# Order of the first block: softmax products ahead of the gate projections, spatial products sooner, six modulation pieces later

## The reference

```
h = rms_norm(x);  q, ckv, qi, ki, wi, u, v, ga, gb = split(h @ w_in)
index = sum_heads(relu(qi . ki) * wi)          # top 64 keys per query
scores = q_lat . c_kv * scale + bias, masked to the chosen keys
o = softmax(scores) @ values;  y_a = o @ w_proj_a
y_b = (gelu(u) * (w_spatial @ layer_norm(gelu(v)) + b_spatial)) @ w_proj_b
x = x + (sigmoid(ga) * y_a + sigmoid(gb) * y_b) @ w_out
x = x + mixture_of_32_experts(rms_norm(x))     # 96 MB of weights
```

## Time and profile before

| | us |
|---|---|
| median of 3 runs | 999.6 |
| lowest, highest | 999.0, 1003.27 |
| profiled execution, its own time | 995.97 |
| its span | 994.2 |
| PE busy | 914.5 (92%) |
| DVE busy | 406.0 (41%) |
| ACT busy | 261.5 (26%) |
| POOL busy | 66.9 (7%) |
| chain that ended last: PE, SP's queue, DMA, DVE | 78%, 10%, 4%, 4% |

### The profile page before, as it was taken

One profiled execution on the slowest core, in us unless ns is written; L12 is line 12 of the kernel. 1 busy time (PEld: TensorE's weight loads), 2 busy tenths in 40 slices (PEclk: granted clock), 3 DMA queues, 4 the chain that ended last, 5 costly groups with the idle time before them and its releaser, 6 DMA issues.

```text
span 994.2 us, 13560 instructions
## 1 busy us (share of the span) xinstructions
PE 914.5 (92%) x5310; PEld 729.6 (73%) x5310; DVE 406.0 (41%) x906; ACT 261.5 (26%) x588; POOL 66.9 (7%) x88
## 2 busy tenths in 40 slices
PE   8889998799999976876799999999999999999997
PEld 7658776688865544443588888788888888878886
DVE  4474555464631211111552461645135236263422
ACT  2244422201322111110327143122111814312201
POOL 5523100002000000000200000000000000000011
PEclk9979999899999988888899999999999999999999
DMA  9935956379999999999463444223334443422311
GB/s 347 371 128 218 374 214 237 143 312 422 371 421 420 422 420 421 421 420 421 165 180 139 168 143 154 103 110 127 128 127 143 175 152 145 169 85 93 136 48 43
DMA packets 35124, 229.52 MB, mean 231 GB/s; under 512 B 5984, under 2 KB 6016, under 8 KB 8176
## 3 DMA queue, kind: packets, MB, share of 16 engines
q1 hardware_dynamic: 30944, 222.05, 57.5%
q0 software_dynamic: 1312, 4.71, 1.3%
q10 hardware_dynamic: 2800, 1.85, 0.6%
HBM read 227.54 MB, written 1.06 MB: 230 GB/s over the span
## 4 chain that ended last, share of the span: by engine, by line
PE 78%; SPq 10%; DMA 4%; DVE 4%; ACT 2%; issue 2%; POOL 0%; DVEq 0%; ACTq 0%; POOLq 0%
PE bank L423 27%; PE bank L1023 11%; SPq L1048 9%; PE bank L886 6%; PE bank L864 6%; PE bank L728 3%; PE bank L629 3%; PE bank L906 3%; DMA s<-in_w_down 3%; PE bank L700 2%; PE bank L743 2%; PE bank L461 2%; PE bank L921 1%; PE bank L987 1%; PE bank L766 1%
## 5 line engine op out<-in xcount | busy, mean ns | idle before, releaser
L423 PE MATMUL bank<-hT,ring 128*128 128x256 f32 x1152 | 261.0, 386 | 1.6 <-DMA ring<-in_first_pieces 1.4
L423 PEld LDWEIGHTS bank<-hT,ring 128*128 128x128 f32 x1152 | 221.0, 194 | 37.1 <-issue 3.4
L1023 PE MATMUL bank<-ring,s 128*128 128x256 f32 x512 | 111.2, 379 | 0.0
L1023 PEld LDWEIGHTS bank<-ring,s 128*128 128x128 f32 x512 | 97.2, 190 | 13.0
L1719 DVE SCALAR_TENSOR_TENSOR z<-z,bank 128x256 f32<-128x256 f32 x9 | 3.8, 421 | 151.5 <-ACT z L1270 151.5
L728 PE MATMUL bank<-s,z 128*32 128x256 f32 (+1 forms) x448 | 45.6, 428 | 15.3 <-DMA s<-in_w_up 4.5
L886 PE MATMUL bank<-ring,hT 128*128 128x256 f32 x256 | 56.4, 380 | 0.0
L728 PE MATMUL bank<-ring,z 128*32 128x256 f32 (+1 forms) x336 | 40.9, 434 | 16.5 <-DMA oth<-in_w_up 6.7
L864 PE MATMUL bank<-hT,ring 128*128 128x256 f32 x256 | 55.6, 379 | 0.0
L886 PEld LDWEIGHTS bank<-ring,hT 128*128 128x128 f32 x256 | 48.4, 190 | 7.2 <-issue 0.9
L864 PEld LDWEIGHTS bank<-hT,ring 128*128 128x128 f32 x256 | 48.5, 190 | 6.5
(11 more groups left out here) (395 smaller groups left out, 1365.0 us busy)
## 6 DMA issues: line engine op xcount, KB each, us to landing
ring<-in_layer_pieces SPq DMA_DIRECT2D x64, 1024.0 KB, 4.8
ring<-in_first_pieces SPq DMA_DIRECT2D x49, 1024.0 KB, 7.4
s<-in_w_gate SPq DMA_DIRECT2D x15, 1024.0 KB, 17.5
s<-in_w_down SPq DMA_DIRECT2D x14, 1024.0 KB, 27.0
s<-in_w_up SPq DMA_DIRECT2D x13, 1024.0 KB, 13.4
ring<-in_w_up SPq DMA_DIRECT2D x11, 1024.0 KB, 19.9
ring<-in_w_gate SPq DMA_DIRECT2D x10, 1024.0 KB, 22.2
ring<-in_w_down SPq DMA_DIRECT2D x9, 1024.0 KB, 23.1
```

What stands on the lines that cost most here:

```text
L423: mm = pe.matmul(b[:, 0:T], w[:, (k0 + kb) * CW + m * P:(k0 + kb) * CW + (m + 1) * P], rhs[:, kb, :], start=(kb == 0), stop=(kb == nk - 1))
L1023: mm = pe.matmul(xo[j, tt][:, 0:CW], yT[:, kb, tt * P:(tt + 1) * P], w[:, kb, :], start=(kh == 0 and kb == 0), stop=(kh == 1 and kb == KB ...
```

## The change

The order of the pieces, the order of PE, ACT and DVE in the loop over heads, and one wait on POOL are changed. No arithmetic is added or taken away. The list of pieces now has no modulation piece behind the q pieces and two behind each v piece. PE does pT ahead of the gate halves of a head and o behind them; gm stands between pT of the last head and the last gate half. ACT copies pT ahead of the exps. DVE does its last modulation piece of the loop behind gmT. POOL waits until all 16 index scores have been added before it multiplies its first piece. ACT's sums of the six pieces move behind u and v.

```diff
--- before.py
+++ after.py
@@ -91,7 +91,9 @@
     tags = [("in", C_QI), ("in", C_QI + CW), left.pop(0), ("latent",), left.pop(0)]
     for c in (C_Q, C_U, C_V, C_GA, C_GB):
         for j in range(2 if c < C_GA else 4):
-            tags += [("in", c + j * CW), left.pop(0)]
+            tags.append(("in", c + j * CW))
+            for _ in range({C_Q: 0, C_U: 1, C_V: 2}.get(c, 1)):
+                tags.append(left.pop(0))
     for j in range(4):
         tags += [("proj", j), left.pop(0)]
     for j in range(4):
@@ -498,7 +500,6 @@
                     for _ in range(4):
                         idx_job()
                 used()
-                ada_job()
                 if j == 0:
                     pe.wait_ge(S["ckv_ready"], 1)
                     b = B.acquire(pe, "cT")
@@ -533,6 +534,7 @@
                     mm.then_inc(A.done, 1)
                 used()
                 ada_job()
+                ada_job()
 
             gate_jobs = [(j, m) for j in range(8) for m in range(2)]
             gst = {}
@@ -551,7 +553,6 @@
             for _ in range(GATES_FIRST):
                 gate_job()
             for h in range(HEADS + 1):
-                gate_job()
                 if h < HEADS:
                     o = (h % 2) * 64
                     for tt in range(TT):
@@ -559,11 +560,8 @@
                         b = B.acquire(pe, f"S{h}{tt}")
                         pe.matmul(b[:, 0:ns], qT[o:o + 64, h // 2, tt * P:(tt + 1) * P], kvT[o:o + 64, h // 2, 0:ns],
                                   start=True, stop=True).then_inc(B.done, 1)
-                if h < GATES_TWICE:
-                    gate_job()
                 if h >= 1:
                     g = h - 1
-                    o = (g % 2) * 64
                     pe.wait_ge(S["prob_ready"], 2 * g + 2)
 
                     b = A.acquire(pe, f"pT{g}")
@@ -571,6 +569,20 @@
                     tr(b[:, 0:P], pn[0][:, 0:P])
                     tr(b[:, P:2 * P], pn[1][:, 0:P])
                     tr(b[:, 2 * P:3 * P], pn[1][:, P:2 * P]).then_inc(A.done, 1)
+                if h == HEADS:
+                    pe.wait_ge(S["vln_ready"], 1)
+                    pe.wait_ge(S["ws_masked"], 1)
+                    for n in range(GROUPS):
+                        b = B.acquire(pe, f"gm{n}")
+                        for c in range(TT):
+                            mm = pe.matmul(b[:, c * P:(c + 1) * P], gv[:, c, n * P:(n + 1) * P], wsT[:, n, :],
+                                           start=True, stop=True)
+                        mm.then_inc(B.done, 1)
+                gate_job()
+                if h < GATES_TWICE:
+                    gate_job()
+                if h >= 1:
+                    o = (g % 2) * 64
                     pe.wait_ge(A.free, A.upto(f"pT{g}"))
                     b = A.acquire(pe, f"o{g}")
                     pe.matmul(b[o:o + 64, 0:P], vnat[:, 0, g * HD:(g + 1) * HD], pT[:, g % 2, 0, :],
@@ -580,15 +592,6 @@
                                        start=(st == 0), stop=(st == 1))
                     mm.then_inc(A.done, 1)
             assert not gate_jobs
-
-            pe.wait_ge(S["vln_ready"], 1)
-            pe.wait_ge(S["ws_masked"], 1)
-            for g in range(GROUPS):
-                b = B.acquire(pe, f"gm{g}")
-                for c in range(TT):
-                    mm = pe.matmul(b[:, c * P:(c + 1) * P], gv[:, c, g * P:(g + 1) * P], wsT[:, g, :],
-                                   start=True, stop=True)
-                mm.then_inc(B.done, 1)
 
             pe.wait_ge(B.free, B.upto("gm3"))
             pe.wait_ge(A.free, A.upto("o7"))
@@ -1171,8 +1174,6 @@
                 out_copy(qT[:, m, :], T)
                 for _ in range(4):
                     idx_job()
-                if m % 2:
-                    ada_job()
             act.wait_ge(S["sp_wanted"], 1)
             step(f(labs, labs, ACT.Exp, scale=-1.0), S["sp_ready"])
             for m in range(4):
@@ -1200,7 +1202,9 @@
             for _ in range(GATES_FIRST):
                 gate_job()
             for h in range(HEADS + 1):
-                gate_job()
+                if h >= 1:
+                    b = A.take(act)
+                    step(f(pT[:, (h - 1) % 2, :, :], b[:, 0:384].rearrange("p (s q) -> p s q", s=3), ACT.Copy), A.free)
                 if h < HEADS:
                     for tt in range(TT):
                         ns = (tt + 1) * P
@@ -1210,13 +1214,12 @@
                             act.wait_ge(A.done, A.upto(f"pT{h - 2}"))
                         step(f(prob[h % 2][tt][:, 0:ns], sc[:, tt, 0:ns], ACT.Exp, bias=rt[:, tt:tt + 1],
                                accum_out=rt[:, 2 + tt:3 + tt]), S["p_ready"])
+                gate_job()
                 if h < GATES_TWICE:
                     gate_job()
                 if h >= 1:
                     g = h - 1
                     o = (g % 2) * 64
-                    b = A.take(act)
-                    step(f(pT[:, g % 2, :, :], b[:, 0:384].rearrange("p (s q) -> p s q", s=3), ACT.Copy), A.free)
                     b = A.take(act)
                     step(f(oaT[o:o + 64, g // 2, :], b[o:o + 64, 0:T], ACT.Copy), A.free)
             assert not gates
@@ -1554,13 +1557,14 @@
                     step(tsc(pn, pn, rt[:, 4 + tt:5 + tt], None, ALU.mult), S["prob_ready"])
                 if h + 1 < HEADS:
                     masked_bias(h + 1)
-                ada_sums(1)
+                    ada_sums(1)
 
             for g in range(GROUPS):
                 b = B.take(v)
                 step(tten(gsum, b[:, 0:T].rearrange("p (c t) -> p c t", c=TT),
                           bsp[:, g, :].unsqueeze(1).broadcast_to([P, TT, P]), ALU.add))
                 step(tten(gmT[:, g, :], gsum.rearrange("p c t -> p (c t)"), guT[:, g, :], ALU.mult), B.free)
+            ada_sums(1)
 
 
             v.wait_ge(S["small_loaded"], 16 * 2)
@@ -2046,6 +2050,7 @@
             g.wait_ge(S["ws_loaded"], 16)
             step(g.affine_select(out=wsT, in_=wsT, compare_op=ALU.is_ge, fill=0.0, base=0,
                                  pattern=[[0, GROUPS], [1, P]], channel_multiplier=-1), S["ws_masked"])
+            g.wait_ge(S["relu_used"], 2 * HEADS)
             ada_sums(ADA_POOL)
             g.wait_ge(S["norm2_loaded"], 16)
             for j in range(4):
```

## The result

The changed kernel takes **984.1 us** (median of 4 runs, 980.9 to 986.2) against 1000.6 for the kernel before (4 runs, 999.0 to 1003.3): a ratio of 0.9829, interval 0.9805 to 0.9854. Its profiled execution took 984.0 us, with a span of 982.3. In a later batch two executions of the kernel before took 1102.1 and 1211.6 us, at a mean granted clock of 0.83 and 0.74 where all others have 0.96 to 0.98; these slow runs are left out of every ratio and median.

A forecast was written before the change was run, and what follows sets the result against it. The expert weight stream was taken to bound the kernel, following PE's first projection P. Shifts of -3.65 (V), +3.1 (supply), +1 (clock) and -14.8 (heads) gave 981.6 us profiled, with 3.6 added 985, range 978 to 993.

The forecast's parts named there:

- What bounds it: Expert stage is paced by its weight stream, which follows PE's first projection P; bringing P forward brings the rest forward.
- swallowed: Rival: the expert stream ends at 469 us whatever PE does, so the time stays at 999.6; chance 0.06.
- Index stretch: Index scores without POOL's multiplications: all 5.18 us of PE idle goes, last index addition moves from 65.15 to 58.2 us.
- One hold: Ahead of V, one POOL multiplication holds a small DVE instruction 4.5 us; V shifts -3.65 us; 985 us, chance 0.50.
- The case of two holds: Rival: a second multiplication also holds DVE's third small instruction, V starts 4.55 us later; 989.5 us, chance 0.27.
- V and u: PE's products V and u take 18.5 us as before, partly at half clock; u ends at 83.75.
- Supply: Before the heads: late loads of v's second and the second gate piece cost +3.1 us, plus +1 for the clock.
- Heads: Loop over heads up to P, reordered: 70.35 us instead of 85.17, so -14.8, ends -11 and -15.5.
- The sum: Whole kernel: -3.65 + 3.1 + 1 - 14.8 = -14.35, so 981.6 us profiled and 985 us median.
- the pieces' half: Moved modulation pieces with POOL's wait, everything outside the heads' reorder: terms -3.65, +3.1 and +1 us.
- The signs: Expected in the trace: POOL's first multiplication about 58.4, V near 65, DMA waits of 1 to 3 us, P near 180.
- the starved rival: Ring supply of v's second and gate pieces lands late, heads start 21 us later; slower, 1006 us, chance 0.05.

The follow-up runs named there:

- sp_wait: Changed kernel with POOL waiting for DVE's third small instruction (`sp_wanted`) instead of the 16th index addition: 976.7 us, ratio 0.9786 to the kernel before.
- pieces_only: Kernel before with only the six modulation pieces moved (new list, POOL's wait, ACT's sums behind u and v), heads' loop as before: 998.9 us, ratio 0.9994.
- lag0: Changed kernel with ACT summing each modulation piece in the call that first reaches it, not one later: 974.6 us, ratio 0.9729 to the kernel before.
- heads_exp_late: Kernel before with only the heads' loop reordered, and ACT's `sp_wanted` wait and small exp moved behind the copies of V: 982.1 us, ratio 0.9825.
- exp_late: Changed kernel with ACT's `sp_wanted` wait and small exp moved from before the copies of K to behind those of V: 971.1 us, ratio 0.9701.
- no_wait: Changed kernel without POOL's wait for the index additions: 979.9 us, ratio 0.9820 to the kernel before.

## Why the prediction was right

985.0 was predicted, 984.1 measured. The mechanism was right. That the two numbers lie so close is in part luck: the prediction worked out 981.6 us for the profiled execution and added 3.6, because the profile before lay that far under its median. The profiled execution took 984.0, so the sum was 2.4 too low; it lay only 0.1 under its median, so the addition was 3.5 too high. Point by point:

- **What bounds it.** P 15.8 us sooner, last landing 14.7 us sooner, median 16.5 us shorter, and over all thirteen profiles the rest keeps its length to some 4 us: the gain was not swallowed.
- **Index stretch.** Last index addition predicted at 58.2, ended at 58.41.
- **One hold.** Predicted: `sp_wanted` at 63.25, V at 65.25. Measured: 63.29, and V at 65.35. K's products end at 58.57 (58.35 predicted). It is the second small instruction that is held, as the sum had it, and the third got through between two multiplications. The case of two holds did not happen here, but sp_wait shows it elsewhere: L1517 and L1518, held by successive multiplications. By the rule of the Trainium skill weighed in the prediction ("SBUF — State Buffer", section "Who interferes with whom") either is possible; these traces show both.
- **V and u.** Predicted 18.5 us, measured from 65.35 to 82.87 17.5. I took the length from before; the clock came back sooner.
- **Supply: mis-sized, and at another place.** I had +3.1 and +1 for the clock, with the wait at the *second* gate piece. Measured: the first gate piece made PE wait, 4.26 us, v's piece 0.85 (predicted 1.8), the second gate piece none. u's end to S0 is 28.0 us for the 26.2 that the two terms give. The step that failed is "the second gate piece is issued only when piece 5 is summed" as the one that sets the heads' start. In the trace the piece for the *first* pair of gate halves is the late one. SP issues in order, and the load ahead of it waits until ACT has summed modulation piece 3, at 92.6 us; then it takes 9.00 us to land. The sum had no term for this piece:

```profile
93.02 9.00 DMA ring<-in_first_pieces
```

- **Heads: mis-sized the other way.** 70.35 predicted, 68.0 measured. A head with two gate halves takes 9.04 us, not 9.35, since the pair runs as one group in 7.07 rather than twice 3.65; one with a single half 5.58, not 5.8. Of the 17.2 us between 85.17 and 68.0, 12.1 - 0.6 = 11.5 is idle time (9.6 at ACT's pT, 2.5 at gm), and 3.4 is clock: two gate halves before took 5.39 and 5.41 us where 3.72 is usual, and none does now. The other 2.3 are joints at which PE no longer stops (pT takes 0.38 us from start to start for 0.49, two gate halves 7.00 for 3.56 + 3.65). The prediction named the clock's effect and put no price on it. In the kernel before, behind a wait of 1.98:

```profile
172.63 0.43 PE L576 MATMUL bank<-s 128*64 128x128 f32 x2 [1.98 <-ACT s L1219]
...
173.43 5.39 PE L423 MATMUL bank<-hT,ring 128*128 128x256 f32 x16
```

- **The sum.** V, u, supply and heads miss by +0.1, -1.0, +1.8 and -2.3: together -1.4 at P, where 180.3 was expected and 178.87 came. The last landing moved 1.1 less than P, and the 2.8 us of clock behind it were not in the sum. The errors cancel in part; the sum was better than its terms.
- **The two halves.** The sum gave the pieces' half -3.65 + 3.1 + 1 = +0.45, that is nothing; pieces_only measures +0.2 at P and a ratio of 0.9994. At S0, where the sum ends, it measures +1.9; the 1.7 that come back in the heads are a slow gate half less, which no term foresaw.
- **The signs.** All named ones came but for the sizes of the two waits on DMA (0.85 and 4.26 where 1 to 3 were named). The heads begin 28.0 us after u's end, well under the 40 of the starved rival.

What stays open: why the first gate piece was slow to land (whether its queue or the traffic beside it) was not tried apart; lag0 shows that an earlier issue is enough. In the heads, PE's new place for pT and ACT's earlier copy of it were not tried apart. Why the clock fell in the two groups of products behind the experts was not followed up.

## What to carry to other kernels

When work is moved out of a stretch by a wait, look at who else the same signal releases: POOL's wait ended just as three tiny instructions, 0.6 us together, were on the critical path, and one signal later the hold fell where nothing waited. In an in-order queue a tiny operation that waits is as costly as its wait; move it behind what the bound engine needs. And a half that measures as nothing can be what lets other edits pay: heads_exp_late moves nothing at P, while the same edit in exp_late takes 1.3% more off the changed kernel.

## What the hardware showed that I had not expected

- A waiting multiplication of POOL gets in between two instructions of DVE that are 0.04 us apart, and then holds the smallest of them for its full length: 128x16 for 4.42 us, 128x2 for 4.18 (L1438). The latter delays a square root on ACT, and its table load waited 1.90 us. MAX8 instructions ran at their usual 0.29 us beside POOL's multiplications: only some kinds are held.
- Idle time and clock don't go together simply. After 6.77 and 4.26 us of idle time the granted clock was 0.50 for a while (V 3.71 us, gate pair 8.86). After 3.04 us (no_wait, gates) and 2.53 (sp_wait, V) it wasn't (7.17 and 1.98), but after 2.52 in no_wait V took 3.49. The stretch after the 6.77:

```profile
66.00:68.00 2.00, 2.00 (x3) 0.67 (x2) 1.79 (x9) 0.99 (x3) 1.92 (x2) 0.50 0.00 0
```

PE is busy for all of it, at 1.2 GHz of its 2.4 (granted clock, the third number from the end). What a wait costs on top of its length is seen best where nothing else changes: V and u take 15.7 us in exp_late, which has no wait there, 17.5 in the changed kernel and 18.5 before, so 1.8 and 2.8 us more.
- The clock also fell where PE had not stood idle: the 16 products of L990 took 4.53 us in the changed kernel's profile (granted clock 0.51 from 632 to 634 us), though PE had been busy throughout the 6 us before, at 1.00. The same products took 2.88 or 2.89 in the twelve others.
